# Modulation chunks in the feed-forward block: half a chunk at a time beside the weight ring, every second chunk on VectorE

## The reference, cut to what matters

```
# first block, its last part
h = rms_norm(x, norm_ffn_pre)
f = (silu(h @ w_ffn_gate) * (h @ w_ffn_up)) @ w_ffn_down
x = x + rms_norm(f, norm_ffn_post)
# second block, its start: w_ada is 1024 x 6144, c one vector of 1024
mod = silu(c) @ w_ada + b_ada
sh1, sc1, g1, sh2, sc2, g2 = split(mod, 6)
h = rms_norm_2(x) * (1 + sc1) + sh1
```

## Time and profile before

| | |
|---|---|
| median of 3 runs | 1145.15 us (1139.17 to 1148.46) |
| the profiled execution's own time | 1143.86 us |
| its span, from the first to the last instruction | 1142.1 us |
| PE busy in the span | 1063.0 us (93%) |
| mean granted clock of PE | 0.989 |

### The profile page before, as it was taken

One profiled execution on the slowest core, in us unless ns is written; L12 is line 12 of the kernel. 1 busy time (PEld: TensorE's weight loads), 2 busy tenths in 40 slices (PEclk: granted clock), 3 DMA queues, 4 the chain that ended last, 5 costly groups with the idle time before them and its releaser, 6 DMA issues.

```text
span 1142.1 us, 17887 instructions
## 1 busy us (share of the span) xinstructions
PE 1063.0 (93%) x7545; PEld 722.8 (63%) x7545; DVE 462.3 (40%) x698; ACT 353.9 (31%) x508; POOL 39.6 (3%) x32
## 2 busy tenths in 40 slices
PE   5999989899999999998999999999899989898986
PEld 4996767789879999886987453434244433242432
DVE  4784244365663534457649261212122212121212
ACT  5742312273454443446543230101011111010102
POOL 0002200000200010000000000000000000000000
PEclk9999999899999999999989999999999999999999
DMA  9454366415645554645465969999999999999994
GB/s 317 157 196 162 105 224 224 150 74 182 205 139 176 188 182 148 239 167 177 147 216 192 371 244 422 420 420 420 421 420 422 421 420 421 420 422 420 420 420 191
DMA packets 95061, 316.31 MB, mean 277 GB/s; under 512 B 7878, under 2 KB 32790, under 8 KB 70294
## 3 DMA queue, kind: packets, MB, share of 16 engines
q1 hardware_dynamic: 93958, 312.70, 71.2%
q10 hardware_dynamic: 1040, 2.69, 0.7%
HBM read 314.32 MB, written 1.05 MB: 276 GB/s over the span
## 4 chain that ended last, share of the span: by engine, by line
PE 71%; DMA 20%; DVE 4%; ACT 2%; issue 2%; SPq 0%; POOL 0%; DVEq 0%; ACTq 0%
DMA arena<-in_w 20%; PE bank L1458 11%; PE bank L751 11%; PE bank L752 11%; PE bank L753 11%; PE bank L1482 4%; PE bank L737 4%; PE bank L1002 3%; PE bank L917 2%; PE bank L1438 1%; PE bank L951 1%; PE bank L728 1%; PE bank L1495 1%; PE bank L698 1%; DVE arena L2544 1%
## 5 line engine op out<-in xcount | busy, mean ns | idle before, releaser
L1458 PE MATMUL bank<-ring,hT 128*64 128x512 f32 x512 | 226.9, 595 | 30.0 <-DMA arena<-in_w 28.8
L1458 PE MATMUL bank<-arena,hT 128*64 128x512 f32 x512 | 226.9, 595 | 0.0
L753 PE MATMUL bank<-h_high,ring_low 128*128 128x256 f32 x688 | 193.5, 281 | 0.0
L1458 PEld LDWEIGHTS bank<-ring,hT 128*64 128x64 f32 x512 | 67.8, 137 | 182.3 <-issue 130.2
L548 DVE TENSOR_TENSOR ring_low<-ring,hi_high 128x2048 fp32r<-128x2048 f32 (+2 forms) x58 | 126.1, 2219 | 102.8 <-ACT hi_high L1629 102.7
L751 PE MATMUL bank<-h_high,hi_high 128*128 128x256 f32 x528 | 150.2, 284 | 0.7 <-DVE h_low L2134 0.7
L752 PE MATMUL bank<-h_low,hi_high 128*128 128x256 f32 x528 | 149.2, 283 | 0.0
L1629 ACT ACTIVATE hi_high<-ring 128x2048 fp32r<-128x2048 f32 (+2 forms) x58 | 104.5, 1855 | 94.4 <-DMA ring<-in_w_ffn_up 35.5
L753 PEld LDWEIGHTS bank<-h_high,ring_low 128*128 128x128 f32 x688 | 130.8, 190 | 0.0
L1482 PE MATMUL bank<-arena 128*64 128x512 f32 x384 | 113.3, 595 | 7.1 <-DVE hT L2756 6.7
L2762 DVE TENSOR_TENSOR arena<-arena,bank 128x512 f32<-128x512 f32 x16 | 17.3, 1084 | 231.1 <-ACT arena L1986 231.1
(11 more groups left out here) (401 smaller groups left out, 1712.7 us busy)
## 6 DMA issues: line engine op xcount, KB each, us to landing
arena<-in_w SPq DMA_DIRECT2D x112, 1024.0 KB, 23.0
ring<-in_w SPq DMA_DIRECT2D x80, 1024.0 KB, 20.5
ring<-in_w_in SPq DMA_DIRECT2D x15, 2048.0 KB, 7.9
ring<-in_w_ada SPq DMA_DIRECT2D x12, 2048.0 KB, 9.2
ring<-in_w_ffn_gate SPq DMA_DIRECT2D x11, 1024.0 KB, 5.5
ring<-in_w_ffn_up SPq DMA_DIRECT2D x11, 1024.0 KB, 8.2
ring<-in_w_ffn_down SPq DMA_DIRECT2D x5, 2048.0 KB, 7.9
ring<-in_w_o SPq DMA_DIRECT2D x2, 2048.0 KB, 7.8
```

Of the source, the lines that this page charges most:

```text
L753: return mm(ps, a[1], b[0], start=False, stop=stop)
L1458: last = mm(both(6 + half, x), hg[:, k, (2 * q + x) * CAP:(2 * q + x + 1) * CAP], w13s[x][k // 4][:, k % 4, half * EF:(half + 1) * EF], st ...
```

## The change

The eight early chunks leave the ring and the recurrence and are worked off in the feed-forward blocks. Turn t (0 to 7, chunk `ADA_EARLY[t]`) belongs to f = 2t+2 and 2t+3. A chunk now comes in two halves of 1 MB into one buffer, `ada_half` (the place of `xn1`, which is free by then); SP issues them behind the load of `("ff", t+3)`: the first when the chunk before is done, the second when the first has been used. Chunks of even turns (`ADA_DVE`) are multiplied on VectorE, four instructions a half, with an accumulator in `junk`; those of odd turns on PE, four matmuls a half. The sum over partitions stays on PE for all, after block 2t+4; for VectorE's chunks it uses -1 in place of 1/32, and the bias is combined by subtraction. Turn 0 in the attention output is replaced by two matmuls of `keep_busy`. The small loads that hung on ring entries `("ada", 0)` and `("ada", 3)` hang on `("gate", 1)` and `("gate", 2)`, and the 1 is added to `modc[:, 8:16]` behind the loop over f.

```diff
 def plan_banks():
-    o += [("o", 0), ("o", 1)] + ada_banks(0) + [("o", 2), ("o", 3)]
+    o += [("o", p) for p in range(PAIRS)]
...
-    o += [("ff", m) for m in range(KF)]
+    for f in range(KF):
+        t = f // 2 - 1
+        o += [("ff", f)] + ([("as", ADA_EARLY[t - 1])] if f % 2 == 0 and 0 < t <= len(ADA_EARLY) else [])
+        o += [("ad", ADA_EARLY[t])] if f % 2 == 0 and 0 <= t < len(ADA_EARLY) and ADA_EARLY[t] not in ADA_DVE else []
...
+ADA_DVE = ADA_EARLY[0::2]
...
-        for c in ADA_EARLY:
-            modulation(c)
...
+                if key[0] == "ff" and 3 <= key[1] < 3 + len(ADA_EARLY):
+                    c = ADA_EARLY[key[1] - 3]
+                    src = cols(A["w_ada_2"][0], c * 512, c * 512 + 512)
+                    if key[1] == 3:
+                        drained(sp, ("hT", 1, 3))
+                    elif c in ADA_DVE:
+                        filled(sp, ("ad", ADA_EARLY[key[1] - 4]))
+                    else:
+                        sp.wait_ge(S("ada_acc"), ADA_DVE.index(ADA_EARLY[key[1] - 4]) + 1)
+                    sp.dma_start(ada_half, src[:, 0:4, :]).then_inc(S("half_full"), 16)
+                    sp.wait_ge(S("half_used"), key[1] - 2)
+                    sp.dma_start(ada_half, src[:, 4:8, :]).then_inc(S("half_full"), 16)
...
             def ada_sum(c):
-                drained(pe, ("ad", c))
+                one = K("thirty_second")
+                if c in ADA_DVE:
+                    one = K("neg_ones")
+                    pe.wait_ge(S("ada_acc"), ADA_DVE.index(c) + 1)
+                else:
+                    drained(pe, ("ad", c))
...
+            def ada_part(t, part):
+                c = ADA_EARLY[t]
+                pe.wait_ge(S("half_full"), 16 * (2 * t + part + 1))
...
+                for j in range(4):
+                    last = mm(ps[32 * j:32 * j + 32, 0:512], cb[:, 4 * part + j, :], ada_half[:, j, :], start=(part == 0),
+                              stop=(part == 1), skip_group_check=True)
...
             for f in range(KF):
...
                 last.then_inc(*full(("ff", f)))
+                t = f // 2 - 1
+                if f % 2 == 0 and 0 < t <= len(ADA_EARLY):
+                    ada_sum(ADA_EARLY[t - 1])
+                if 0 <= t < len(ADA_EARLY) and ADA_EARLY[t] not in ADA_DVE:
+                    ada_part(t, f % 2)
...
             for f in range(KF):
+                if f % 2 == 0 and 0 < f // 2 - 1 <= len(ADA_EARLY) and ADA_EARLY[f // 2 - 2] not in ADA_DVE:
+                    ada_rows(ADA_EARLY[f // 2 - 2])
                 ps = filled(act, ("ff", f))
...
+            def ada_products(t, part):
+                c, acc = ADA_EARLY[t], modp[ADA_EARLY[t]]
+                dve.wait_ge(S("half_full"), 16 * (2 * t + part + 1))
+                if part:
+                    dve.wait_ge(S("half_used"), t + 1)
+                for j in range(4):
+                    k = 4 * part + j
+                    if k == 0:
+                        ins = V.tensor_scalar(acc, ada_half[:, j, :], csil[:, k:k + 1], None, ALU.mult)
+                    else:
+                        ins = V.scalar_tensor_tensor(acc, ada_half[:, j, :], csil[:, k:k + 1], acc, ALU.mult, ALU.add)
+                    if j < 3:
+                        link(ins)
+                    else:
+                        ins.then_inc(S("ada_acc") if part else S("half_used"), 1)
...
                 V.tensor_tensor(fT[:, f, :], sil[:, f % 2, :], ps[:, SEQ:2 * SEQ], ALU.mult).then_inc(*free(("ff", f)))
+                if f % 2 == 0 and 0 < f // 2 - 1 <= len(ADA_EARLY):
+                    ada_sum(ADA_EARLY[f // 2 - 2])
                 if f % 2:
                     low_parts(N_FF + f // 2 + 3)
+                if 0 <= f // 2 - 1 < len(ADA_EARLY) and ADA_EARLY[f // 2 - 1] in ADA_DVE:
+                    ada_products(f // 2 - 1, f % 2)
```

More of the change, by code:

```diff
@@ L165 @@
 PARCOL, PARBLOCK = par_columns()
-def ada_banks(turn):
-    return ([("as", ADA_EARLY[turn - 1])] if turn else []) + ([("ad", ADA_EARLY[turn])] if turn < len(ADA_EARLY) else [])
 def plan_banks():
@@ L608, in _ @@
                     sp.dma_start(B("lvlf"), A["levels"]).then_inc(S("lvl_in"), 16)
-                if key == ("ada", 3):
+                if key == ("gate", 2):
                     bcast(dtb, A["dt_bias_2"][0], "router_in")
@@ L890, in ada_sum @@
                     for k in range(KD):
-                        last = mm(ps[o:o + 64, k:k + 1], modp[c][:, 64 * k:64 * k + 64], K("thirty_second")[:, 0:1],
+                        last = mm(ps[o:o + 64, k:k + 1], modp[c][:, 64 * k:64 * k + 64], one[:, 0:1],
                                   start=True, stop=True)
@@ L894, in ada_sum @@
                     for j in range(4):
-                        last = mm(ps[:, j:j + 1], modp[c][:, j * P:(j + 1) * P], K("thirty_second")[:, 0:1],
+                        last = mm(ps[:, j:j + 1], modp[c][:, j * P:(j + 1) * P], one[:, 0:1],
                                   start=True, stop=True)
                 else:
-                    last = mm(ps[:, 0:512], K("thirty_second"), modp[c], start=True, stop=True)
+                    last = mm(ps[:, 0:512], one, modp[c], start=True, stop=True)
                 last.then_inc(*full(("as", c)))
-            def ada(turn):
-                if turn:
-                    ada_sum(ADA_EARLY[turn - 1])
-                if turn < len(ADA_EARLY):
-                    ada_chunk(ADA_EARLY[turn])
+            def ada_part(t, part):
+                c = ADA_EARLY[t]
+                pe.wait_ge(S("half_full"), 16 * (2 * t + part + 1))
+                if part == 0:
+                    pe.wait_ge(S("cb"), 1)
+                    ps = write(pe, ("ad", c))
+                else:
+                    ps = bank[BANK["ad", c][0]]
+                for j in range(4):
+                    last = mm(ps[32 * j:32 * j + 32, 0:512], cb[:, 4 * part + j, :], ada_half[:, j, :], start=(part == 0),
+                              stop=(part == 1), skip_group_check=True)
+                if part == 0:
+                    last.then_inc(S("half_used"), 1)
+                else:
+                    last.then_inc(*full(("ad", c)))
             def ada_chunk(c):
@@ L965, in _ @@
                 if p == 2:
-                    ada(0)
+                    keep_busy(write(pe, ("o", p)), 2)
                 pe.wait_ge(S("att_w"), p // 2 + 1)
@@ L1006, in _ @@
                 grams(i, q)
-            ada(1)
             for i, q in both:
@@ L1020, in _ @@
                     group(("x", i, lv, q), q, lambda h, r: gm[r, i, h, 0:CH], lambda h, r: dd[r, i, h, :])
-                ada(lv + 1)
                 for i, q in both:
@@ L1031, in _ @@
                 group(("w1", i, q), q, lambda h, r: gm[r, i, h, 2 * CH:3 * CH], lambda h, r: vp[r, i, h, :])
-            ada(LEVELS + 1)
             for i, q in both:
@@ L1036, in _ @@
                 group(("u", i, q), q, lambda h, r: ddT[r, i, h, :], lambda h, r: zb[r, i, h, :], P)
-            ada(LEVELS + 2)
             def at(p):
@@ L2366, in _ @@
             state_out(2)
-            for c in (2, 3):
-                drained(dve, ("as", c))
-            V.tensor_scalar(modc[:, 8:16], modc[:, 8:16], 1.0, None, ALU.add).then_inc(S("mod"), 1)
             for i in range(NT):
@@ L2435, in _ @@
                 V.tensor_tensor(fT[:, f, :], sil[:, f % 2, :], ps[:, SEQ:2 * SEQ], ALU.mult).then_inc(*free(("ff", f)))
+                if f % 2 == 0 and 0 < f // 2 - 1 <= len(ADA_EARLY):
+                    ada_sum(ADA_EARLY[f // 2 - 2])
                 if f % 2:
                     low_parts(N_FF + f // 2 + 3)
+                if 0 <= f // 2 - 1 < len(ADA_EARLY) and ADA_EARLY[f // 2 - 1] in ADA_DVE:
+                    ada_products(f // 2 - 1, f % 2)
+            for c in (2, 3):
+                drained(dve, ("as", c))
+            V.tensor_scalar(modc[:, 8:16], modc[:, 8:16], 1.0, None, ALU.add).then_inc(S("mod"), 1)
             for n in range(N_FF + KF // 2 + 3, BY_TWO):
```

34 lines of the change are left out of this document (14 added, 20 removed).

## The result

The median goes from 1146.8 us (1139.17 to 1148.95) to 1240.6 us (1239.95 to 1241.8): 1.083 times the time before (95% interval 1.078 to 1.089). The forecast was 1251, range 1222 to 1290. The profiled span goes from 1142.1 to 1239.5 us.

A forecast was written before the change was run, and what follows sets the result against it. The prediction took PE's own work to bound the recurrence and feed-forward blocks. Span 1142.1 + 124.1 (feed-forward) + 10 (clock) - 28 (recurrence) = 1248.2; with 1.8 and 1.3 for the median, 1251 us, range 1222 to 1290.

The forecast's parts named there:

- Gain in the recurrence: Recurrence, 143 to 227 us: sums and chunk products leave PE, most stops and low clock go; 28 us, bounds 20 and 32.
- The stops: Recurrence: PE's five bare stops laid to "issue", 6.8 us in all, counted within the gain, taken to go mostly.
- The products: Feed-forward blocks, VectorE: four products take 2.5 us for a first half and 2.8 for a second, at 0.7 and 0.4.
- The loop: Feed-forward blocks: from VectorE's release of a first half to its next, two chunks later, 52.2 us; PE has four blocks in it.
- The end of the stage: Feed-forward blocks after three turns: last accumulation, PE's last chunk, 12.3 us until ScalarE's release, last sum, three blocks; ends at 251 us.
- The stage: Feed-forward blocks grow from 126.7 to 251 us, by 124.1 with 16 us of added work, plus 10 for the clock.
- The clock: Feed-forward blocks: low PE clock after long waits costs up to 20 us over four turns; 10 taken.
- first release: Feed-forward blocks: VectorE first releases a first half 30.0 us after the stage begins.
- three turns: Feed-forward blocks: three loop turns of 52.2 us after the first release bring the time to 186.6 us.
- Low clock throughout: Rival: PE stays at 1.2 GHz from the first wait to the end of the feed-forward stage; 1304 us, chance 0.08.
- The waits: Feed-forward blocks: PE waits 23 then 14 us at VectorE chunks' sums, 4 at a first half, 7 at its own sums.
- The cause: Feed-forward blocks: order makes load, low part and products follow each other; VectorE has room for some 24 us of added work.

The follow-up runs named there:

- best_again: Changed kernel with two half buffers, all eight chunks on VectorE ahead of the low part, each sum one block later: 1126.2 us, 0.984 of before.
- products_first: Changed kernel with VectorE's four products of a second half put ahead of the low part of the same odd block: 1195.6 us, 1.046 of before.
- small_chunk_loads: Kernel before, each of the eight early chunk loads cut to one of eight row groups, PE's work the same: 1135.8 us, 0.993 of before.
- no_chunks_in_ff: Changed kernel without the eight early chunks' halves, products and sums in the feed-forward blocks: 1111.9 us, 0.973 of before.
- two_buffers_first: Changed kernel with a second half buffer, VectorE's products ahead of the low part and ScalarE's copies ahead of the high part: 1162.1 us, 1.018.
- two_half_buffers: Changed kernel with a second buffer for second halves, programs of PE, ScalarE and VectorE in their old order: 1220.3 us, 1.068 of before.

## Why the prediction was right

- **Gain in the recurrence.** 28 said. From the start of the grams to the ring load at the end of block 1 it is 337.21 - 143.15 = 194.1 us before and 307.88 - 144.81 = 163.1 after: 31.0. The stops (6.8 to 2.2 us) and the clock (0.94 to 1.00) came as said.
- **The products.** 2.5 and 2.8 us a half said, 2.8 and 3.1 measured: 751 ns each in place of the 0.7, 478 in place of 0.4.
- **The loop.** 52.2 us a turn said, before clock, and 2.5 for the clock. SP issues a second half as soon as VectorE has released the first, at 325.85, 378.91, 433.85 and 490.84: turns of 53.1, 54.9 and 57.0 us. The first came 29.7 us after the stage began (296.1 us), 30.0 said. One step read otherwise than written: from the second turn on, the ring load did not follow the release at once but 4.8, 4.7 and 3.3 us later, when PE's block ended. Most of that was made up before the products, since the steps up to SP's next first half together take 22.5, 23.1 and 21.3 us where 21.1 were said.
- **The end of the stage.** This is the term that was too large. From the last release to the end of the stage 251 - 186.6 = 64.4 us were said, without the clock; 60.5 were measured, with it. The 12.3 us up to ScalarE's release of the last sum were 7.6 (525.84 to 533.39): I took a load of two megabytes there, 8 us and a high part of 3.7, but it is the `ffn_down` piece of one, which the earlier trace rows list beside the others. Its high part takes 2.0 us:

```profile
530.90 2.01 ACT L1654 ACTIVATE hi_high<-ring 128x1024 fp32r<-128x1024 f32 x2 [3.42 <-DMA ring<-in_w_ffn_down]
532.81 0.58 ACT L1768 ACTIVATE arena<-bank 128x512 f32<-128x512 f32 x1
```

- **The stage.** 255.2 - 127.0 = 128.2 us more, and 124.1 + 10 said. The clock was nearly right: about 8 us on the loop, as worked out above, for the 10. With that, 251.0 said for the stage become 255.2 measured as -0.3 (first release), +1.8 (three turns, about what longer products make), +8.2 (clock) and -5.5 (end of the stage). The clock fell to 0.50 in each long wait and stayed there 6 to 10 us after PE resumed, and much of that was in blocks with slack: PE's busy time held some 24 us of it. Low clock throughout (1304) did not come: it was back at 1.00 in each turn. (That rival's 12 us a turn are 47 in four, not 46.)
- **The waits.** 23 then 14 at VectorE's sums said, 21.7 then 12.1 to 12.7; 4 at half products, 3.1 to 3.3; 7 at PE's own sums, 5.7 to 7.1, but at the last one 0.8, for the reason just given.
- **The cause.** "It is the order that costs", not the capacity, was the point of the argument. That capacity does not bind is shown: `best_again` does more work on VectorE and is faster than before. That the order costs is shown for the part that `products_first` gave back, 45 of 94 us with nothing else moved. It is not the whole: of the 126 us by which the stretch grew, both reorderings take off 51, the second buffer with them 31 more, and all chunks on VectorE with later sums 34 more. The rule of the Trainium skill that I cited (Trainium Kernel Development and Optimization, Best Practices) is borne out only in part: the second buffer alone took 23 us off the stretch, the order alone 51. A buffer helps where its release is early.
- **The sum.** A span of 1248.2 said, 1239.5 measured; 1142.1 + 128.2 - 31.0 is 1239.3, so the two terms seem to leave nothing over. That they meet so closely is chance: the grams began 1.7 us later, the two terms overlap by 0.4, and what follows the stage is 1.9 us shorter. 5.9 us of the difference are in the stage and 3.0 in the recurrence; the other 2 of 1251 against 1240.6 are what I added to the span for the median.

## What to carry to other kernels

When transfers are issued by one queue in program order, write down the loop that each wait in that queue closes: who releases it, and what stands ahead of the release on that engine. A product behind a step that needs the next load makes load and work follow each other, even where the engines have room: here VectorE was busy 83 of 255 us. Price such a loop turn by turn; it gave the time here to 1%. Look at the last turn by itself, since it can have other loads than the rest. And move the release ahead before adding a buffer: here that was worth more, and each made the other worth more.

## What the runs showed of the hardware

**VectorE and GpSimd.** In `best_again` the same product takes 0.75 us or up to 1.87. VectorE's products in 377 to 382 us (minimum, median, maximum):

```profile
L2344 DVE SCALAR_TENSOR_TENSOR arena<-arena,small x5: 747/752/1867, 376.3 to 380.9; 128x512 f32<-128x512 f32 x5
```

GpSimd's time line there:

```profile
378.22 1.28 POOL L2099 TENSOR_TENSOR f_low<-arena,f_high 128x512 fp32r<-128x512 f32 x1 [12.49 <-ACT f_high L1850]
```

One product in this second half meets GpSimd's `f_low`, 1.28 us, and ends 1.1 us later. Where the two meet otherwise GpSimd's instruction gets longer too (1.60 us at 391.19). The group's mean is 896 ns there, 751 in the changed kernel, where the two never met. The Trainium skill (SBUF — State Buffer, Who interferes with whom) says that a VectorE instruction with two SBUF inputs contends with a GpSimd instruction that reads SBUF, and calls the ports that the two engines share an exclusive lock. These rows agree with it: the product grew by nearly the length of `f_low`.

**Stops of PE with a full DMA queue.** `small_chunk_loads` shows that some 8 us of a kernel bound by PE hung on the bytes of loads that PE did not wait for. The trace also shows beside what the stops stand. The profile has a DMA queue of the kind "instruction", 50 packets of 16 KB in the kernel before, and one of them lies in the longest stop (163.06 to 166.00), among 204 packets of the loads. The DMA view of 163.5 to 165 us:

```profile
q1 hardware_dynamic: 204, 0.39, 70.8%
q8 instruction: 1, 0.02, 4.6%
```

By its start and length in the packed trace that packet ends at 164.76, and PE goes on 1.24 us later. It is so at every stop laid to "issue" between 143 and 227 us: six in the kernel before, with the one of 0.16 us, end 1.24 to 1.59 us after such a packet, and the one of `small_chunk_loads` ends 1.34 us after one. In the changed kernel four of the five short stops there do too (1.32 to 1.76 us after), one of 0.39 us does not. This speaks for PE waiting for its own instructions, which come over the same DMA engines as the weights; it is an inference from the times, as no run moved these packets alone.

**Quicker blocks.** Two feed-forward blocks take 11.52 us before, in `small_chunk_loads` (331.72 to 343.24) and, ahead of the first chunk, in `best_again` (306.44 to 317.96), but 11.31 in `no_chunks_in_ff`:

```profile
316.35 0.37 SPq L618 DMA_DIRECT2D ring<-in_w_ffn_gate  x1
327.65 0.37 SPq L618 DMA_DIRECT2D ring<-in_w_ffn_gate  x1
338.96 0.37 SPq L618 DMA_DIRECT2D ring<-in_w_ffn_gate  x1
```

with the same 96 matmuls between them, clock 1.00 and no wait in either. It is 2.3 us if all 22 blocks have it. The chunks in the blocks do not explain it: `two_buffers_first` takes 11.31 us for the same two blocks (306.90 to 318.21) and `two_half_buffers` 11.52 (306.32 to 317.84). Both paces also occur in one execution: in the changed kernel the L760 rows follow each other every 0.353 us from 304 to 312 us, every 0.360 from 440 to 443 and every 0.353 again at 530. The cause stays open; cutting the bytes of the loads did not bring it.
